# Attention scores over 64 rows, two heads in turn, and a later request for the residual rows

## What is computed

```python
h = rmsnorm(x, g_mix)
q, k, v, u, qm = split(h @ w_in)             # 8 heads of 64; u: 256 pooling channels; qm: 4 heads of 64
y_attn = three dilated windows (128,1) (512,4) (2048,16) with ALiBi, merged by their softmax denominators
y_pool = (trailing means of 2, 4, 8, 16 positions - u) @ w_pool * pool_scale
y_mem  = softmax(qm @ km.T / 8) @ vm         # 256 memory tokens
x = x + concat(y_attn, y_pool, y_mem) @ w_out
h2 = rmsnorm(x, g_ffn)
x = x + relu(h2 @ w_ff1) ** 2 @ w_ff2        # 1024 -> 4096 -> 1024
return rmsnorm(x, g_final)
```

## Time and profile before

| | before |
|---|---|
| median of 3 runs | 1740.71 us (1736.01 to 1760.82) |
| profiled execution | 1757.16 us |
| span of its slowest core, core 4 | 1756.1 us |
| spans of the other cores | 1715.7 to 1744.7 us |
| PE matmul busy | 1619.6 us, 92% |
| DVE busy | 995.3 us, 57% |
| ACT busy | 754.8 us, 43% |
| granted PE clock, core 4 | 0.962 of full |

### The profile page before, as it was taken

The page is one execution under the profiler, slowest core; times in us unless marked ns, Lnnn a source line. Parts: engine busy times, 40 slices in busy tenths (PEclk is TensorE's granted clock), DMA queues, the critical chain, the costliest instruction groups (busy, mean ns, idle before and its releaser), DMA issues.

```text
span 1756.1 us, 30507 instructions; the slowest of 8 cores (1715.7 to 1756.1 us)
## 1 busy us (share of the span) xinstructions
PE 1619.6 (92%) x10320; PEld 859.1 (49%) x10320; DVE 995.3 (57%) x1613; ACT 754.8 (43%) x1481; POOL 59.4 (3%) x103
## 2 busy tenths in 40 slices
PE   4896786799999999999999989999899999999897
PEld 2455443454445544554455535554455545554443
DVE  4657454444656556755566555655566565655434
ACT  3427613345235552556245542555145633445112
POOL 2000000000000000000000000000000000000000
PEclk9999898888899999999999999999999999999899
DMA  9999999943553366333734464324633263235243
GB/s 219 240 181 187 165 205 187 178 126 109 180 186 109 121 211 195 141 133 123 230 123 156 145 207 148 144 109 142 248 113 149 100 240 138 97 121 203 108 156 120
DMA packets 67927, 280.68 MB, mean 160 GB/s; under 512 B 6080, under 2 KB 25792, under 8 KB 45120
## 3 DMA queue, kind: packets, MB, share of 16 engines
q1 hardware_dynamic: 37008, 215.19, 36.0%
q0 software_dynamic: 30768, 63.54, 18.5%
HBM read 278.09 MB, written 39.85 MB: 181 GB/s over the span
## 4 chain that ended last, share of the span: by engine, by line
PE 78%; DMA 10%; DVE 5%; issue 3%; ACT 3%; DVEq 0%; SPq 0%; ACTq 0%; POOL 0%; POOLq 0%
PE mm L447 31%; PE mm L869 22%; DMA ring<-wscratch 8%; PE sc L447 7%; PE ob L703 6%; PE sc L675 6%; PE sc L810 3%; PE tp L424 2%; DMA x<-xh 2%; PE mm L810 1%; ACT tmp L400 1%; DVE x L875 1%; DVE hb L414 1%; ACT P L677 1%; DVE x L836 1%
## 5 line engine op out<-in xcount | busy, mean ns | idle before, releaser
L447 PE MATMUL mm<-h2T,ring 128*128 128x512 bf16 x2080 | 498.9, 386 | 23.6 <-DVE qmB L584 11.9
L869 PE MATMUL mm<-ring,aT 128*128 128x512 bf16 x2048 | 487.8, 385 | 26.6 <-DMA ring<-wscratch 17.1
L677 ACT ACTIVATE P<-sc 128x512 bf16<-128x512 f32 x487 | 283.2, 595 | 257.7 <-PE sc L675 242.8
L857 DVE TENSOR_TENSOR aT<-tmp 128x512 bf16<-128x512 f32 x256 | 176.9, 691 | 268.6 <-ACT tmp L856 267.7
L869 PEld LDWEIGHTS mm<-ring,aT 128*128 128x128 bf16 x2048 | 194.4, 99 | 245.8 <-issue 69.7
L447 PEld LDWEIGHTS mm<-h2T,ring 128*128 128x128 bf16 x2080 | 198.0, 99 | 237.2 <-issue 52.1
L856 ACT ACTIVATE tmp<-mm 128x512 f32<-128x512 f32 x256 | 152.8, 597 | 347.1 <-PE mm L447 325.2
L875 DVE TENSOR_TENSOR x<-x,mm 128x512 f32<-128x512 f32 x256 | 174.9, 686 | 163.2 <-PE mm L869 159.0
L686 DVE TENSOR_TENSOR P<-P,E 128x512 bf16<-128x512 bf16 x448 | 185.9, 421 | 65.4 <-ACT P L677 63.8
L703 PE MATMUL ob<-P,Vd 128*128 128x128 bf16 x1792 | 178.0, 223 | 13.0 <-DVE P L686 12.9
L400 ACT ACTIVATE tmp<-x 128x1024 bf16<-128x1024 f32 x80 | 84.5, 1056 | 164.1 <-DVE x L815 77.2
(11 more groups left out here) (99 smaller groups left out, 1213.4 us busy)
## 6 DMA issues: line engine op xcount, KB each, us to landing
ring<-wscratch SPq DMA_DIRECT2D x173, 1024.0 KB, 6.5
wscratch<-w_ff POOLq DMA_DIRECT2D x16, 1024.0 KB, 142.1
out<-x POOLq DMA_DIRECT2D x32, 512.0 KB, 4.5
x<-xh SPq DMA_DIRECT2D x28, 512.0 KB, 20.2
xa<-xh POOLq DMA_DIRECT2D x20, 512.0 KB, 5.3
x<-xh POOLq DMA_DIRECT2D x20, 512.0 KB, 8.6
Vd<-Vd SPq DMA_DIRECT2D x33, 192.0 KB, 5.8
xa<-xh SPq DMA_DIRECT2D x12, 512.0 KB, 14.8
```

The lines of the kernel that those rows point to most:

```text
L447: T.op("pe", lambda: nc.tensor.matmul(out_ap, lhsT=l, rhs=r, start=(i == 0), stop=(i == n - 1)), reads=reads, writes=[b_out], mark=(i == n ...
L677: T.op("act", lambda: nc.scalar.activation(out=P_[:], in_=s_, func=AF.Exp, bias=bt.get("bias", 0.0)), reads=[bs_], writes=[bP_])
L857: T.op("dve", lambda: nc.vector.tensor_tensor(out=aT[:, fl, :], in0=rt[:], in1=rt[:], op=ALU.mult), reads=[brt], writes=[b_aT[fl]])
L869: T.op("pe", lambda: nc.tensor.matmul(m_[:], lhsT=aT[:, fl, tc * 128:(tc + 1) * 128], rhs=pf[:, fl % 4, ch * 512:(ch + 1) * 512], start=(f ...
```

## The change

Queries are stored once, with 0.125 on all rows. A score matmul takes 64 rows of KT and of QA: 0 to 63 for the even head, 64 to 127 for the odd one. Batches are paired, head 2i with head 2i+1, and the eight (or two) score matmuls of a pair are issued in turn, one of each head, into two sc tiles. Of 66 items still, the even ones (item0) do the front of a pair and the back of the even head's batch of the pair before, and the odd ones (item1) only the back of the odd head's batch. Both ob tiles are thus in use by one pair of heads, and both change heads together. The lag is one pair in every tile. load_x1 for tc 0 to 2 moves from the head of slot_mix behind MLP group 30 (tile 4 keeps its place at 34).

```diff
-                            in0=m_[:, :].rearrange("p (c r) -> p r c", r=4), scalar1=csm_t[:, 5:6], scalar2=None,
+                            in0=m_[:, :].rearrange("p (c r) -> p r c", r=4), scalar1=0.125, scalar2=None,
                             op0=ALU.mult),
-                            reads=[bm_, b_g], writes=[b_Q])
-                        T.op("dve", lambda: nc.vector.tensor_scalar(
-                            out=QB[:, ol, :].rearrange("p (r c) -> p r c", r=4),
...
-                Qz = (QA if hh == 0 else QB)[:, pr, :]
+                p0 = 64 * hh
+                Qz = QA[p0:p0 + 64, pr, :]
...
-                        kv = KT[:, pr, slot * TOK:(slot + 1) * TOK].rearrange("p (a s) -> p a s", s=4)[:, :, r]
+                        kv = KT[p0:p0 + 64, pr, slot * TOK:(slot + 1) * TOK].rearrange("p (a s) -> p a s", s=4)[:, :, r]
...
+                n = len(bts[0]["qk"])
+                for i in range(n):
+                    for bt, s_, bs_ in fr:
+                        sec, l, r = bt["qk"][i]
...
+                        T.op("pe", lambda: nc.tensor.matmul(o2, lhsT=l, rhs=r, start=True, stop=True),
+                             reads=bt["qk_reads"], writes=[bs_], mark=(i == n - 1))
+                for bt, s_, bs_ in fr:
+                    P_, bP_ = bt["P"]
+                    T.op("act", lambda: nc.scalar.activation(out=P_[:], in_=s_, func=AF.Exp, bias=bt.get("bias", 0.0)),
+                         reads=[bs_], writes=[bP_])
...
+            for i in range(n + 1):
+                def item0(i=i):
                     if i < n:
-                        emit_front(batches[i])
+                        emit_front(pairs[i])
                     flush_post()
-                    if i >= lag:
-                        emit_back(batches[i - lag])
-                items.append(item)
+                    if i >= 1:
+                        emit_back(pairs[i - 1][0])
+
+                def item1(i=i):
+                    flush_post()
+                    if i >= 1:
+                        emit_back(pairs[i - 1][1])
+                items += [item0, item1]
...
-            if not first:
-                for tc in range(3):
-                    load_x1(j, tc)
...
+                if not first and g == 30:
+                    for tc in range(3):
+                        load_x1(j, tc)
```

More of the change, by code:

```diff
@@ L175, in build_nc @@
         QA = sb("QA", [128, 4, TOK], BF16)
-        QB = sb("QB", [128, 4, TOK], BF16)
         b_Q = Buf("Q")
         qmA = sb("qmA", [128, 2, TOK], BF16)
-        qmB = sb("qmB", [128, 2, TOK], BF16)
         b_qm = Buf("qm")
@@ L562, in stage_B @@
                             out=QA[:, ol, :].rearrange("p (r c) -> p r c", r=4),
-                            in0=m_[:, :].rearrange("p (c r) -> p r c", r=4), scalar1=csm_t[:, 5:6], scalar2=None,
+                            in0=m_[:, :].rearrange("p (c r) -> p r c", r=4), scalar1=0.125, scalar2=None,
                             op0=ALU.mult),
-                            reads=[bm_, b_g], writes=[b_Q])
-                        T.op("dve", lambda: nc.vector.tensor_scalar(
-                            out=QB[:, ol, :].rearrange("p (r c) -> p r c", r=4),
-                            in0=m_[:, :].rearrange("p (c r) -> p r c", r=4), scalar1=csm_t[:, 6:7], scalar2=None,
-                            op0=ALU.mult),
-                            reads=[bm_, b_g], writes=[b_Q])
+                            reads=[bm_], writes=[b_Q])
                     elif pi == 1:
@@ L580, in stage_B @@
                             out=qmA[:, mp, :].rearrange("p (r c) -> p r c", r=4),
-                            in0=m_[:, :].rearrange("p (c r) -> p r c", r=4), scalar1=csm_t[:, 5:6], scalar2=None,
+                            in0=m_[:, :].rearrange("p (c r) -> p r c", r=4), scalar1=0.125, scalar2=None,
                             op0=ALU.mult),
[L583 to L588, removed]
+                            reads=[bm_], writes=[b_qm])
                 if own and (j > NHALO or ip == 0):
@@ L605, in flush_post, with attn_items @@
                 posts.pop(0)()
-        def attn_items(j, lag, nsc):
+        def attn_items(j, nsc):
             batches = []
@@ L636, in attn_items @@
                         if qb == 0:
-                            kprev = KT[:, pr, prv * TOK + 384: prv * TOK + 512]
+                            kprev = KT[p0:p0 + 64, pr, prv * TOK + 384: prv * TOK + 512]
                         else:
-                            kprev = KT[:, pr, cur * TOK + (qb - 1) * 128: cur * TOK + qb * 128]
-                        ksame = KT[:, pr, cur * TOK + qb * 128: cur * TOK + (qb + 1) * 128]
+                            kprev = KT[p0:p0 + 64, pr, cur * TOK + (qb - 1) * 128: cur * TOK + qb * 128]
+                        ksame = KT[p0:p0 + 64, pr, cur * TOK + qb * 128: cur * TOK + (qb + 1) * 128]
                         oo = o_[:, :, 32 * qb:32 * qb + 32]
@@ L653, in attn_items @@
                 mp, hh = mh // 2, mh % 2
-                Qz = (qmA if hh == 0 else qmB)[:, mp, :]
+                p0 = 64 * hh
+                Qz = qmA[p0:p0 + 64, mp, :]
                 v0 = mp * 192 + 64 * hh
                 for kc in range(2):
-                    batches.append(dict(qk=[(None, kmT[:, mp, kc * 128:(kc + 1) * 128], Qz)],
+                    batches.append(dict(qk=[(None, kmT[p0:p0 + 64, mp, kc * 128:(kc + 1) * 128], Qz)],
                                         qk_reads=[b_km, b_qm], mask=None, meng=None,
@@ L661, in attn_items @@
                                         post=(6 + mh // 2, hh) if kc == 1 else None))
[L663 to L685, removed]
@@ new lines, in emit_front @@
+            def emit_front(bts):
+                fr = []
+                for bt in bts:
+                    si = cnt["sc"] % nsc
+                    cnt["sc"] += 1
+                    pi = cnt["P"] % NPB
+                    cnt["P"] += 1
+                    bt["P"] = (Pbuf[pi], b_P[pi])
+                    fr.append((bt, scb[si], b_sc[si]))
+                n = len(bts[0]["qk"])
+                for i in range(n):
+                    for bt, s_, bs_ in fr:
+                        sec, l, r = bt["qk"][i]
+                        o2 = s_[:, sec, :] if sec is not None else s_.rearrange("p a b -> p (a b)")
+                        if len(r.shape) == 3:
+                            o2 = o2.rearrange("p (a b) -> p a b", a=r.shape[1])
+                        T.op("pe", lambda: nc.tensor.matmul(o2, lhsT=l, rhs=r, start=True, stop=True),
[4 more added lines that the diff above has]
+                         reads=[bs_], writes=[bP_])
+                    if bt["mask"] is not None:
+                        m = bt["mask"]
+                        Pv = P_[:].rearrange("p (a b) q -> p a b q", a=2) if len(m.shape) == 4 else P_[:]
@@ L686, in emit_front @@
                         T.op("dve", lambda: nc.vector.tensor_tensor(out=Pv, in0=Pv, in1=m, op=ALU.mult),
                              reads=[bP_, b_E], writes=[bP_])
-                bt["P"] = (P_, bP_)
             def emit_back(bt):
@@ L720, in emit_back @@
                     reads=[bo_, brc], writes=[b_yT[ychunk]]))
+            pairs = []
+            for a in range(6):
+                half = 7 if a < 4 else 2
+                base = 14 * a if a < 4 else 56 + 4 * (a - 4)
+                for i in range(half):
+                    pairs.append((batches[base + i], batches[base + half + i]))
             items = []
-            n = len(batches)
-            for i in range(n + lag):
-                def item(i=i):
+            n = len(pairs)
+            for i in range(n + 1):
+                def item0(i=i):
                     if i < n:
-                        emit_front(batches[i])
+                        emit_front(pairs[i])
                     flush_post()
-                    if i >= lag:
-                        emit_back(batches[i - lag])
-                items.append(item)
+                    if i >= 1:
[5 more added lines that the diff above has]
+                items += [item0, item1]
             return items
@@ L897, in slot_mix @@
             first = (j == NHALO)
-            if not first:
-                for tc in range(3):
-                    load_x1(j, tc)
-            lag = 3 if first else 2
-            at = attn_items(j, lag, 5 if first else 3)
+            at = attn_items(j, 5 if first else 3)
             pool_ops = stage_pool(j)
```

## The result

The changed kernel takes 1798.09 us against 1739.89 before: ratio 1.0323, 95% interval 1.0283 to 1.0362, 56 us slower. The forecast was 1722, with a range that ended at 1792. The profiled execution took 1798.01 us, 41 us more than that of before, which had run 16 us above its median.

A forecast was written before the change was run, and what follows sets the result against it. PE was taken as the bound from 344 us on, full DMA engines before. Terms -46 + 0 + 43 - 6 - 5 - 5 = -19 us, so 1741 - 19 = 1722 us; range 1692 to 1792.

The forecast's parts named there:

- Scores: Score matmuls in slot_mix: a pair's two heads run side by side, saving 7.0 us a slot, 46 us over 6.6 slots.
- Changing between 128 and 64 rows: PE's 64 changes a slot between full- and half-height matmuls cost 0; other end 0.16 us each, 68 us.
- drain at each change: Rival: heads overlap but the array empties 64 times a slot in slot_mix, +49, 1790 us; chance 0.18.
- The ob tiles: PE waits in slot_mix for ob tiles handed over together: 6.5 us a slot, 43 us over 6.6 slots.
- Tile 4 is covered: What tile 4 and the first part of tile 5 save or lose is covered by the DMA queue: 0.
- Queries once: First MLP group of slot_mix waits only for qmA, 0.86 us earlier in seven tiles: 6 us off.
- residual rows: Later requests save 5 us of waiting for the second output-projection piece over five tiles, and 5 us in tile 5.

The follow-up runs named there:

- run 16: Not a run label: the words say that the profiled execution of the kernel before had run 16 us above its median.
- e9: Changed kernel with the multiplication freeing the odd head's ob ahead of the new pair's front, and items over 62 MLP groups instead of 58; ratio 0.9979, 1736 us.
- e10: e9 with full-height scores over 128 rows and the zero-padded queries; ratio 1.0041 to the kernel before, 1747 us.
- e1: Changed kernel with the VectorE multiplication that frees the odd head's ob put ahead of the new pair's front, not behind its masks; ratio 1.0154, 1767 us.
- e2: Changed kernel with full-height scores over all 128 rows and the zero-padded QA and QB of before; ratio 1.0344 to the kernel before, 1800 us.
- e3: Kernel before with queries stored once and scores over 64 rows, one head at a time, no pairs; ratio 1.0517, 1830 us.
- e4: Kernel before with only the residual-row requests (tc 0 to 2) moved behind MLP group 30; ratio 0.9952, 1732 us.
- e8: Changed kernel with the residual-row requests back at the head of slot_mix; ratio 1.0413 to the kernel before, 1812 us.

## Why the prediction was wrong

Taken against 1740, the forecast was -19 and the result +56. By its own steps:

- **Scores, -46: right.** Eight half-height scores take about the time of four. Full overlap was the right pick, and two weight loads do fit into 55 ns.
- **Changing between 128 and 64 rows, 0: this is the step that failed.** I took the value of the nearest rows, where changes of columns and of tiles cost nothing, and held the 0.16 of an emptied array for the far end. It is 0.12 in and 0.11 out. 64 x 0.115 x 6.6 = 49 us, and the scores' gain is gone. The rows show it as a weight load that starts only with its matmul. The Trainium skill, "TensorEngine Tiling (Array Packing)", section Key Properties, says that changing the tiling mode drains TensorE. The trace agrees that such a change costs time, 0.12 and 0.11 us; whether the array empties or only the weight load is held back, no run here tells apart. e9 and e10 say the same in another way: scores that should save 7.0 us a slot by overlap save 0.1. The rival "drain at each change" gave 1790 for 0.16 a change, and named 0.13 as the point from which it decides; at 0.115 it alone would have ended at 1771.
- **The ob tiles, +43: right, with a part left out.** 47.7 us, and the chain at group 14 has the queue order worked out; e1, which moves one instruction, shows that these waits cost time and don't only stand where PE would wait anyway. Left out was the clock: after the longest holes, at group 14 in five tiles and at group 50 in two, most of the next group runs at the lower level, 10 us in all.
- **Tile 4 is covered, 0: wrong.** Its ob waits were 15.7 us (4.7 before). The first ring request in its output projection comes at 223.06 us instead of 214.38, 8.7 us later. The windows of tile 4's slot_mix, before first, then the changed kernel, then e2 and e3:

```profile
134.00:213.00 79.00, 53.49 (x541) 38.44 (x540) 49.92 (x100) 55.92 (x106) 3.13 (x4) 0.87 1.02 179
```

```profile
134.00:223.00 89.00, 59.12 (x538) 35.48 (x537) 49.19 (x96) 55.96 (x106) 4.70 (x6) 0.69 1.04 170
```

```profile
134.00:214.00 80.00, 47.30 (x507) 38.26 (x506) 47.16 (x94) 53.34 (x102) 3.13 (x4) 0.84 1.03 177
```

```profile
134.00:212.00 78.00, 72.11 (x498) 43.66 (x500) 44.31 (x90) 56.64 (x104) 3.13 (x4) 0.52 1.03 173
```

  The DMA engines are as full in all four. In the changed kernel the granted clock went from 0.87 to 0.69, but the clock alone isn't the reason for the delay: e2, pairs with full-height scores, has 0.84 and comes 9.6 us later than before, with 16.7 us of waits for ob in this slot. e3, half-height scores without pairs, has 0.52 and 2.3 us of waits for ob, and comes 9.1 us later. Each of the two changes thus delays tile 4 by itself, and both together do it by 10.0; why they don't add up isn't shown. The next ring pieces are requested when PE lets go of a buffer, and the slot of tile 5 doesn't give the 10 us back: it is 2.6 us shorter, and the late residual rows alone make it 6.7 shorter. A full DMA system didn't absorb a PE that asks later. What the forecast said of tile 5 itself, that about 0.6 of a slot counts there, came out: 6.7 - 2.6 = 4.1 us, half of the 8.2 of a later slot. The 91 of 91 us in the earlier trace rows on which it rested were taken at a granted clock of 0.80, but core 0, at 1.00, was busy 82.75 of 84 us from 346 us on.
- **Queries once, -6, and residual rows, -10: right in size** (waits 11.9 to 6.1; e4 -8, e8 +16). The place of the second was half wrong: all of it is in tile 5, 6.7 us, and no gain can be told at the output projection.

Sum: -46 + 49 + 48 + 10 + 9 - 6 - 10 = +54, against +56. Missing from the forecast were 49 us of changes of rows, 5 us of waits for ob, and 19 us for the clock behind PE's holes and for tile 4. The slots test most of the terms: over tiles 6 to 11 they give -42 + 44 + 41 + 10 - 5 = +48, and the eight cores show +49.4, between 1050.5 and 1099.9. That the whole comes within 2 us is still partly luck. The clock's 10 us are those of core 4 (other cores have fewer low stretches), and the 0.16 us behind each of the 42 waits for ob, up to 7 us, stand in no term.

## What to carry to other kernels

Count the places where TensorE goes between full and half rows. With 0.23 us for there and back and 55 ns for a 128-column matmul, four matmuls saved pay for one round trip. By this estimate half-height pairs pay only in longer runs than this kernel's eight; no run here had a longer one. Before pairing two accumulators, ask when each is handed over: two that change hands together have nothing to work behind, and an instruction that frees a buffer belongs ahead of work that waits. The hole of 2.6 us at group 14 cost another 1.65 us because the clock fell behind it. And time that a full DMA queue should cover has to be checked there: tile 4's 10 us were not covered.

## What was not expected of the hardware

- Half-height matmuls of the two row halves ran side by side even when the queue held four of one half and then four of the other (0.36 us for eight, against 0.34 for four of one half alone).
- At a change between 128 and 64 rows no weight load was brought forward, in either direction, and the changes cost 0.12 and 0.11 us.
- One hole with PE busy for 0.70 of 3 us was followed by a stretch at a granted clock of 0.57 (3.38 us for a group of 1.73).
